# Inverse roots of the heads' outputs, second layer: from ScalarE's logarithm and exponential to bit arithmetic and Newton steps on VectorE

## The reference

```python
def rms_norm(x, g):
    xf = x.astype(jnp.float32)
    y = xf * lax.rsqrt(jnp.mean(xf * xf, -1, keepdims=True) + EPS)
    return (y * g.astype(jnp.float32)).astype(x.dtype)

def diff_mixer(...):                       # 8 heads, two maps each, d = 64
    ...
        p = jax.nn.softmax(sc, -1)
        a = (p[:, :, 0] - lam * p[:, :, 1]).astype(v.dtype)
        return jnp.einsum('bhqk,bkhd->bqhd', a, v)
    o = merge_blocks(...)
    o = rms_norm(o, subln_g) * (1.0 - lam_init)      # per token and head, over 128 columns
    return o.reshape(b, s, H * 2 * d) @ w_o
```

## Time and profile before

| what | value |
|---|---|
| median of 3 runs | 1344.09 us (1343.32 to 1346.96) |
| the profiled execution | 1345.34 us, of which the span is 1343.5 us |
| TensorE busy | 1282.8 us (95%) |
| ScalarE busy | 548.0 us (41%) |
| VectorE busy | 509.6 us (38%) |
| differential attention, first scores to last output product | about 356 to 453 us from the span's start |

### The profile page before, as it was taken

How to read it: one execution, slowest core, us unless ns; L and a number is a source line. 1 busy time by engine, 2 the same in 40 slices (tenths; PEclk the granted TensorE clock), 3 DMA queues, 4 the chain that set the end, 5 groups by cost and what they waited for, 6 DMA issues and landing times.

```text
span 1343.5 us, 20032 instructions
## 1 busy us (share of the span) xinstructions
PE 1282.8 (95%) x7959; PEld 954.6 (71%) x7959; DVE 509.6 (38%) x1303; ACT 548.0 (41%) x853; POOL 573.2 (43%) x136
## 2 busy tenths in 40 slices
PE   6999999999998899999999999999999999999996
PEld 6867999998987799999878888854444444454442
DVE  2434444445265454444657453421111111121112
ACT  4654555556477465555543664311111111111112
POOL 4722788885944188888567855200000000000001
PEclk9999999999999999999999999999999999999998
DMA  8731666664633266664446444599999999999994
GB/s 270 235 94 63 182 195 188 190 199 144 220 126 95 63 203 196 196 188 165 149 165 203 159 137 161 230 421 426 427 428 428 429 428 429 429 429 428 429 423 189
DMA packets 156933, 341.22 MB, mean 254 GB/s; under 512 B 8537, under 2 KB 119482, under 8 KB 144314
## 3 DMA queue, kind: packets, MB, share of 16 engines
q1 hardware_dynamic: 156858, 340.18, 68.1%
HBM read 339.10 MB, written 1.05 MB: 253 GB/s over the span
## 4 chain that ended last, share of the span: by engine, by line
PE 75%; DMA 13%; ACT 4%; DVE 4%; POOL 2%; issue 1%; SPq 0%; ACTq 0%; DVEq 0%
PE bank L669 16%; PE bank L671 15%; PE bank L670 15%; PE bank L1237 11%; DMA xspare<-in_w 6%; DMA ring<-in_w 6%; PE bank L1262 5%; PE bank L1187 3%; PE bank L768 2%; POOL parts L621 2%; PE bank L679 1%; PE bank L1217 1%; ACT parts L1305 1%; PE bank L1105 1%; PE bank L1121 1%
## 5 line engine op out<-in xcount | busy, mean ns | idle before, releaser
L621 POOL TENSOR_TENSOR parts<-raw,parts 128x2048 fp32r<-128x2048 f32 (+4 forms) x128 | 568.0, 4466 | 290.2 <-ACT parts L1305 290.2
L669 PE MATMUL bank<-xh,parts 128*128 128x256 f32 x1032 | 288.0, 279 | 6.0 <-POOL parts L621 4.0
L670 PE MATMUL bank<-xl,parts 128*128 128x256 f32 x1032 | 285.9, 277 | 0.0
L671 PE MATMUL bank<-xh,parts 128*128 128x256 f32 x1032 | 285.8, 277 | 0.0
L1305 ACT ACTIVATE parts<-raw 128x2048 fp32r<-128x2048 f32 (+4 forms) x128 | 236.1, 1853 | 23.4 <-PE bank L669 8.5
L1237 PE MATMUL bank<-ring,room 128*64 128x512 f32 x768 | 226.1, 594 | 7.1 <-DMA ring<-in_w 4.5
L644 POOL TENSOR_TENSOR xn<-h,gpost 128x512 f32<-128x512 f32 x4 | 4.9, 1270 | 474.7 <-DVE h L2258 474.7
L669 PEld LDWEIGHTS bank<-xh,parts 128*128 128x128 f32 x1032 | 194.2, 188 | 12.6 <-POOL parts L621 4.8
L670 PEld LDWEIGHTS bank<-xl,parts 128*128 128x128 f32 x1032 | 193.8, 188 | 0.8
L671 PEld LDWEIGHTS bank<-xh,parts 128*128 128x128 f32 x1032 | 193.9, 188 | 0.0
L1237 PEld LDWEIGHTS bank<-ring,room 128*64 128x64 f32 x768 | 72.5, 137 | 111.4 <-issue 111.4
(11 more groups left out here) (255 smaller groups left out, 1858.9 us busy)
## 6 DMA issues: line engine op xcount, KB each, us to landing
ring<-in_w SPq DMA_DIRECT2D x67, 2048.0 KB, 22.9
raw<-in_ffn_w_up SPq DMA_DIRECT2D x88, 512.0 KB, 4.9
room<-in_w SPq DMA_DIRECT2D x12, 2048.0 KB, 20.3
raw<-in_ffn_w_down SPq DMA_DIRECT2D x44, 512.0 KB, 3.9
xspare<-in_w SPq DMA_DIRECT2D x11, 2048.0 KB, 26.6
raw<-in_w_in SPq DMA_DIRECT2D x40, 512.0 KB, 4.1
raw<-in_diff_w_qkv SPq DMA_DIRECT2D x24, 512.0 KB, 4.6
ring<-in_w SPq DMA_DIRECT2D x10, 1024.0 KB, 24.8
```

The lines of the kernel that those rows point to most:

```text
L621: pool.tensor_tensor(low[:, p % PARTS, 0:n], raw[:, p % RING, 0:n], high[:, p % PARTS, 0:n], ALU.subtract).then_inc(low_ready, 1)
L669: first = pe.matmul(out_, a[0], b[0], start=start, stop=False)
L670: pe.matmul(out_, a[0], b[1], start=False, stop=False)
L671: return first, pe.matmul(out_, a[1], b[0], start=False, stop=stop)
```

## The change

ScalarE no longer makes the logarithm and the exponential after the sums of squares; the semaphore `logged` and four increments of `guessed` go with them. VectorE no longer calls `refined` for the pairs, but `inverse_roots`: mean and epsilon, a shift right and a subtraction from a constant on the value's bits, the factor -0.5, and three Newton steps of three instructions. All are on four columns at once, and each is followed by a `link`.

```diff
@@ head_out (ScalarE)
                         squares(ss_o[:, at:at + 1], b[:, P * x:P * x + P], score[:, x // 2, P * (x % 2):P * (x % 2) + P],
                                 pair_squares)
-                    act.wait_ge(pair_squares, 2 * (hd + 1))
-                    r = rs_o[:, 2 * hd - 2:2 * hd + 2]
-                    act.activation(r, ss_o[:, 2 * hd - 2:2 * hd + 2], ACT.Ln, bias=eps_t[:, 0:1],
-                                   scale=1.0 / P).then_inc(logged, 1)
-                    act.wait_ge(logged, hd // 2 + 1)
-                    act.activation(r, r, ACT.Exp, scale=-0.5).then_inc(guessed, 1)
@@ (VectorE)
+            def inverse_roots(y, sums):
+                v, a = st[:, 32:36], st[:, 48:52]
+                link(dve.tensor_scalar(v, sums, 1.0 / P, EPS, ALU.mult, ALU.add))
+                link(dve.tensor_scalar(y.bitcast(I32), v.bitcast(I32), 1, None, ALU.logical_shift_right))
+                link(dve.tensor_scalar(y.bitcast(I32), y.bitcast(I32), -1.0, float(0x5f3759df), ALU.mult, ALU.add))
+                link(dve.tensor_scalar(v, v, -0.5, None, ALU.mult))
+                for _ in range(3):
+                    link(dve.tensor_tensor(a, y, y, ALU.mult))
+                    link(dve.tensor_tensor(a, a, v, ALU.mult))
+                    link(dve.scalar_tensor_tensor(y, a, 1.5, y, ALU.add, ALU.mult))
             def outputs_scaled(m):
                 dve.wait_ge(pair_squares, 4 * m + 4)
                 r = rs_o[:, 4 * m:4 * m + 4]
-                refined(r, ss_o[:, 4 * m:4 * m + 4], P, 4)
+                inverse_roots(r, ss_o[:, 4 * m:4 * m + 4])
```

More of the change, by code:

```diff
@@ L349, in build @@
         neg_max, exped, probs = sem("neg_max"), sem("exped"), sem("probs")
-        pair_squares, logged = sem("pair_squares"), sem("logged")
+        pair_squares = sem("pair_squares")
         o_ready, scored, diag_ready = sem("o_ready"), sem("scored"), sem("diag_ready")
```

## The result

| | before | after |
|---|---|---|
| median | 1345.53 us (1343.32 to 1350.77, 4 runs) | 1360.26 us (1358.51 to 1364.31, 4 runs) |
| ratio after / before | | 1.0109, interval 1.0084 to 1.0133 |
| the profiled execution | 1345.34 us, span 1343.5 | 1360.09 us, span 1358.3 |

The change makes the kernel 1.1% slower, 14.7 us. The forecast was no change, and even the rival that named the right sign gave 1348.5 at most.

A forecast was written before the change was run, and what follows sets the result against it. The prediction took TensorE as the bound, with VectorE's scaled pairs setting two of its attention starts. Terms of +0.78, +0.78, -1.10, -0.10 and -0.36 summed to 0.0 us, giving 1344.1 us, range 1340.9 to 1347.0.

The forecast's parts named there:

- Pair by pair: Attention, on TensorE's clock: shifts of +0.78, +0.78, -1.10, -0.10 and -0.36 us, summing to 0.0 us.
- What comes to VectorE: Roots of each pair: 13 linked instructions at 0.20 us, 2.60 us instead of 1.82, so +0.78 per pair.
- What goes from ScalarE: Per pair two table loads and two activations, 3.0 us, about 12 us of ScalarE in all; loads not needed again.
- rival C: ScalarE's table loads stay because the compiler puts some elsewhere: 1344.8 us, chance 0.03.
- What bounds the kernel now: TensorE, busy 95%; VectorE's scaling of the pair, not ScalarE, sets its starts at 401.84 and 420.22.
- rival A: ScalarE, as the profile's chain of waits says, holds TensorE at 401.84: 1338.5 us, chance 0.10.
- Pair 0: Attention, step 5: VectorE works without pause to the scaled pair, so TensorE starts at 402.62 instead of 401.84, +0.78 us.
- Pair 2: Attention: VectorE's 2.86 us wait goes and the scaled pair comes 2.1 us earlier, worth -0.10 us at most to TensorE.
- Pair 3: Attention: the scaled pair comes 2.1 us earlier and TensorE's 0.36 us idle before 443.22 goes, -0.36 us.
- Step 8: Attention: TensorE's idle 3.10 us shrinks to 2.0, resuming at 425.35; the shift falls from 1.56 to +0.46 us.
- The clock: TensorE's two half-clock stretches in the attention, up to 1.6 us each, taken as unchanged; gains or losses put in the range.
- Rival B: Longer waits at TensorE's starts at 402.6 and 421.8 bring half-clock stretches, 1.6 us each: up to 1348.5 us, chance 0.07.

## Why the prediction was wrong, point by point

**The step that failed** is the sentence in the sum "Pair by pair": "GpSimd's low parts and SyncE's loads come up to 3 us earlier and wait no one off." I gave GpSimd's work beside the new roots a price of nothing and named no work that hid it. I looked for who waits on GpSimd, and by semaphores no one does. I did not look at what runs beside it. The runs showed a price of 2.9, 3.0 and 4.3 us of hold-up on VectorE in pairs 0 to 2, and the slow clock behind the longer idle times. That GpSimd comes 3 us earlier is not what costs: with the activations kept it comes as late as before, and the growth is +10.4 against +10.6. With the hold-up removed, by a wait on GpSimd, the ratio is 0.9993 against a forecast of no change.

**What comes to VectorE.** 2.60 us was right where nothing holds it up: 2.57 with GpSimd's waits, 2.60 in pair 3 of the kernel after. The most that the sum allowed for a small instruction, 0.27 us, was too small by a factor of 16 (4.45). I took it from rows in which GpSimd was at rest. The trace of before has rows that would have warned me, at the very end. VectorE's timeline there:

```profile
1335.94 1.22 DVE L2297 TENSOR_TENSOR st<-st 128x2 f32<-128x2 f32 x1 [0.89 <-ACT room L1316]
```

GpSimd's:

```profile
1333.42 4.94 POOL L644 TENSOR_TENSOR xn<-h,gpost 128x512 f32<-128x512 f32 x4 [474.73 <-DVE h L2258]
```

Two columns in 1.22 us, beside four GpSimd instructions of 128x512 in 4.94, which is 1.24 each. It ends at 1337.16, and by their mean length the third of the four ends at about 1337.1. That a small linked row can be this much longer I had never asked. The bound of the range should have been GpSimd's whole instruction, 4.55 us for each pair.

**What goes from ScalarE.** Right in amount: 11.9 us by the page, and no loads come back (rival C falls). What the sum missed is that ScalarE's earlier piece starts GpSimd earlier, and that decides which root instruction is held up and for how long. It is not what costs the time: the attention grows by as much with the activations kept.

**What bounds the kernel now** was read rightly. TensorE's starts in steps 5 and 7 follow the scaled pair by 0.14 us in the kernel after, 404.88 + 0.69 = 405.57 and 405.71, though the activations are gone, and the old roots without the activations leave TensorE's 1.59 us as they were: rival A falls.

**Pair by pair.** Pair 0 was to be +0.78 and was +3.7, pair 1 the same; the difference is the hold-up, 2.9 and 3.0 us. Pair 2 was to gain 0.1 and cost 2.7: its 4.29 us of hold-up are 2.2 longer than the 2.1 that the removed wait gave, and its sums came 0.45 later by the slow clock after 436. Pair 3, the only one unhindered, did what was forecast: the idle 0.36 us before its transposes is gone. Step 8 was to take 1.10 off the delay through a shorter idle time of 2.0; it fell to 1.66, but the slow clock used that up.

**The clock.** Rival B's mechanism was right and too small. It named 2.3 us of idle time as perhaps enough for a new half-clock stretch, and with the idle times of 2.34 and 2.28 each start did bring one. With 5.3 us the slow clock costs more: over 400 to 410 the granted clock was 0.74 in the kernel after and 0.83 in the one with GpSimd's waits, and over 430 to 440 it was 0.56. B's price of 1.6 each belongs to the short idle times. The length of the idle time does not decide alone: in the kernel after, 2.49 us before 446.83 brought no slow clock (the eight products took 1.13 us), and in the kernel before 1.56 did at 445.44 and 1.59 at 401.84 did not. What else it takes is not shown here.

## What to carry to other kernels

When a change puts new instructions on an engine, lay each of them beside what runs on the others at that moment, also where no semaphore ties them together: an instruction can be held up with no wait in the profile, as busy time. Before small operations are put on VectorE while GpSimd streams large ones, look at their forms: in the probes a one-column tensor_scalar, a PSUM operand, a reduce or a reciprocal ran through; a tensor_scalar on two to four columns or any two SBUF inputs didn't. Where that can't be had, a wait on GpSimd cost nothing here (0.9993), since its results were not due soon, and shorter GpSimd instructions didn't help. Keeping the intermediate values of the roots in PSUM, which the probes suggest as a way out, was not run.

## What the runs showed of the hardware

An instruction on four columns of VectorE took 4.45 us beside a GpSimd subtraction of 4.57, against 0.16 alone, and ended 0.02 to 0.03 us behind it each time. With the form alone changed, from one column to two, the price went from 0.15 to 3.22 us. In the other direction GpSimd's 4.49 us became 6.51. Beside a GpSimd fill, which only writes, the two-input form ran through and the tensor_scalar didn't. Two halves of GpSimd's work let one VectorE instruction through between them and shut the next one out, 0.94 and then 2.27 us.
